# Splitting the probabilities and values of one attention branch into high and low parts

## The chip, the cores and the metric

The kernel runs on one core of one Trainium2 chip, in float32. The metric is the device time of one execution in microseconds (us); lower is better. The engines are TensorE (PE; PEld is its weight load), VectorE (DVE), ScalarE (ACT), GpSimd (POOL) and SyncE (SP), which here only issues DMAs. In the profile a matmul on float32r operands shows one weight load and one matmul, a matmul on float32 operands shows two of each, which are called two passes here.

## The reference

One layer of a streaming encoder on 1024 prompt tokens and 64 sample tokens, model width 1024. Two attention branches read one input projection; branch A is what is changed:

```python
_, idx = lax.top_k(score, topk)
k_sel = jax.vmap(lambda kb, ib: kb[ib])(k_all, idx)
v_sel = jax.vmap(lambda vb, ib: vb[ib])(v_all, idx)
...
logits = (jnp.einsum('bthd,btkd->bthk', qa, k_sel).astype(jnp.float32) * (HEAD_DIM ** -0.5)
          + jnp.moveaxis(bias, -1, 2))
logits = jnp.where(valid[:, :, None, :], logits, NEG_INF)
probs = jax.nn.softmax(logits, axis=-1).astype(v_sel.dtype)
return jnp.einsum('bthk,btkd->bthd', probs, v_sel)
```

Branch A has 8 query heads of width 64 that share one K and one V; each query keeps its 256 best keys. Branch B is a sliding-window attention with 8 heads. After them come the gates, the output projection, and a feed-forward block of width 4096.

## The kernel before

The kernel works in stages: input normalisation, indexer and top-k, input projection, branch A, branch B, output projection, feed-forward, final norm. Each engine has one instruction stream in program order, with semaphores between them.

Branch A is a list of units (`attention_units`). For each pair of heads there are 13: units 0 to 3 are head 0 with query blocks 4 to 7 (5 to 8 key tiles of 128), units 4 to 7 are both heads with blocks 0 to 3 (2, 4, 6, 8 tiles), units 8 to 11 are head 1 with blocks 4 to 7, and unit 12 is the sample block of both heads (17 tiles: 16 of the cache and one of its own). A pair so has 89 tiles, branch A has 4 pairs, 52 units and 356 tiles. Units are counted from 0 within a pair below.

For a unit, TensorE makes the logits (`logits`), VectorE adds the bias and finds the row maximum in one instruction (L1807), negates the maximum (L1820), ScalarE takes the exponential with that maximum as bias (`probs`, L1423), TensorE turns the probabilities with the identity in groups of up to four tiles (`turn_probs`, L1082) into PSUM bank 4 or 5, the turned group is copied to SBUF (`copy_turned`: even groups VectorE L1835, odd groups ScalarE L1439), TensorE multiplies it with the values (`weigh`, L1091; the turned probabilities are the stationary operand, the 64 value columns the moving one, both float32), and VectorE divides by the row sum into `y_tok` (`normalised`, L1868 to L1876).

In the loop iteration of unit n, TensorE turns unit n, makes the logits of unit n + 3, and weighs unit n - 1 (in the iteration of a sample unit, also that unit). A turn needs its PSUM bank free (`turn_read`), and a group is weighed when it has been copied. VectorE copies unit n, adds the bias for unit n + 3, takes the reciprocal of unit n, and normalises unit n - 1. ScalarE copies unit n and takes the exponential of unit n + 2.

The queries come through one buffer, `q_raw`, one head at a time. SyncE loads head hh (`load_q`, L500) when GpSimd has finished with the head before; ScalarE rounds it (`q_hi`, L1415) in its iterations of units 3 and 6 of a pair, at their end; GpSimd subtracts that from `q_raw` (L785) and so frees the buffer. GpSimd's loop over the 16 heads waits for nothing else within the first half of a pair.

At the end of the input projection VectorE copies the turned K and V rows out of PSUM into `kv_tok` (L1758), which TensorE waits for one group of products later (`beside_last`).

Of the kernel before, what the change touches and what calls it, by code (L numbers as in the profile page):

```python
# [5 lines left out]
F32 = mybir.dt.float32  # L6
# [7 lines left out]
P = 128  # L14
# [129 lines left out]
def hybrid_step(nc, x_prompt, x_sample, cache_k_a, cache_v_a, cache_kidx, cache_k_win, cache_v_win,  # L144
# [4 lines left out]
    with ExitStack() as ctx:  # L149
# [128 lines left out]
        probT = [at(f"probT{s}", [P, 4 * P], F32, B + (15168, 15680, 14016, 14528)[s]) for s in range(4)]  # L278
# [214 lines left out]
        def _(sp):  # L493
# [107 lines left out]
            def load_bias_a(pair):  # L601

                for half in range(2):
                    hh = 2 * pair + half
                    if pair:

                        sp.wait_ge(sem("biased"), starts[pair - 1] + (8, 12)[half])
# [3 lines left out]
            def load_bias_s(pair):  # L611

                if pair:
                    sp.wait_ge(sem("biased"), starts[pair])
# [28 lines left out]
            for dst_p, dst_s, tok, c0 in ((k_a_p, k_a_s, kv_tok, 0), (v_a_p, v_a_s, kv_tok, HD)):  # L643
                sp.dma_start(rows(dst_p), tok[:, 0:NBLK, c0:c0 + HD]).then_inc(stored, 16)
                sp.dma_start(dst_s[0, 0], tok[0:DEC, NBLK, c0:c0 + HD]).then_inc(stored, 16)
# [95 lines left out]
            sp.wait_ge(sem("out_stored"), 16 * 12)  # L741
# [3 lines left out]
        def _(pl):  # L745
# [36 lines left out]
            for hh in range(16):  # L782
# [5 lines left out]
                if hh % 2 == 1:  # L788
# [6 lines left out]
                    pl.wait_ge(sem("q_pair_done"), hh + 1)  # L795
            splits(4, 2, dmas=2)
# [5 lines left out]
        def _(pe):  # L802
# [211 lines left out]
            for name, v in (("tok_done", 4), ("kA_lo_done", 1), ("mask_ready", 1), ("cacheV_in", 16), ("cacheA_in", 32)):  # L1014
                pe.wait_ge(sem(name), v)
# [48 lines left out]
            def values(u, kb):  # L1064

                own = u["w"] - P * kb < P
                if u["br"] == "a":
                    tok = kv_tok[:, kb if u["blk"] is not None else NBLK, HD:P]
                    return tok[0:DEC] if own else (tok if u["blk"] is not None else cacheV[:, kb, :])
# [25 lines left out]
            def turn_outputs(pair, part):  # L1095
                pe.wait_ge(sem("y_done"), starts[pair + 1])
                for g, tl in units[starts[pair + 1] - 1]["turn"][part:part + 1]:
# [7 lines left out]
            def turn_outputs_a(n, pair, part):  # L1105

                pe.wait_ge(sem("y_done"), n - 1)
                for m, t in enumerate(units[starts[pair + 1] - 1]["turn"][part][1]):
# [13 lines left out]
            def weigh_all(u):  # L1122
# [7 lines left out]
                if u["n"] < 4:  # L1130
                    pe.wait_ge(sem("kAS_lo_done"), u["n"] + 1)
                for k, (g, before, tiles) in enumerate(groups):
# [127 lines left out]
        def _(ac):  # L1260
# [156 lines left out]
            def probs(u):  # L1417

                s = ring(u)
                ac.wait_ge(sem("biased"), u["n"] + 1)  # L1420
# [10 lines left out]
            def copy_turned(g, before, n):  # L1431

                if g % 2 == 0:
                    return
                ac.wait_ge(sem("turned1"), g // 2 + 1)
                free = before - 1 if g < a_groups else before
                if free > 0:
                    ac.wait_ge(sem("probT_used1"), free)
                ac.activation(probT[slot_of(g, before)][:, 0:n], bank(5, n), ACT.Copy).then_inc(sem("turn_read1"), 1)  # L1439

            def turn_hi_a(n, pair, part):

                if pair == 0 and part == 0:
                    ac.wait_ge(sem("out_stored"), 16 * 12)
# [106 lines left out]
        def _(dv):  # L1551
# [204 lines left out]
            for m, tok in ((0, kv_tok), (2, vb_tok)):  # L1756
                dv.wait_ge(sem("tok_turned"), m + 1)
                dv.tensor_copy(tok[:, 0:NBLK, :].rearrange("p t c -> p (t c)"), bank(6, 1024)).then_inc(sem("tok_done"), 1)  # L1758
                dv.wait_ge(sem("tok_turned"), m + 2)
                if m == 0:  # L1760
                    dv.tensor_copy(kb_tok[:, 0, :], bank(6)[:, P:2 * P])
# [10 lines left out]
            def inverse(u):  # L1772
# [3 lines left out]
                total = den if u["br"] == "b" else rsum  # L1776
# [287 lines left out]
```

## Time and profile before

| | us |
|---|---|
| median of 3 runs | 1857.34 (1856.16 to 1857.66) |
| the profiled execution | 1856.75 |
| its span, first to last instruction | 1854.8 |
| PE busy in the span | 1791.3 |
| DVE busy | 940.5 |
| ACT busy | 644.9 |
| POOL busy | 470.3 |

The span is what the profile covers; the rest of the profiled execution's time lies around it. Branch A takes the stretch from about 520 to 710 us. An engine's busy time says how long it had an instruction in work; whether it set the end is read from the stretch at issue.

### The profile page before, as it was taken

How to read it: one execution, taken by the hardware profiler on the slowest of the kernel's cores; microseconds unless marked ns; L12 is line 12 of the kernel's file. 1: busy time of each engine (PE TensorE's matmuls, PEld its weight loads, DVE VectorE, ACT ScalarE, POOL GpSimd, SP SyncE). 2: the span in 40 equal slices, each digit the busy share in tenths (PEclk: the TensorE clock that was granted, in tenths of full speed). 3: DMA queues.
4: the chain of work that ended last, by engine and by line, in shares of the span. 5: the costliest groups of instructions: out<-in, count | busy, mean ns of one | idle time of the engine just before them, and what ended most of it. 6: DMA issues, size and time to landing. Idle time of an engine off the chain costs nothing.

```text
span 1854.8 us, 30253 instructions
## 1 busy us (share of the span) xinstructions
PE 1791.3 (97%) x11176; PEld 1706.9 (92%) x11176; DVE 940.5 (51%) x2291; ACT 644.9 (35%) x1254; POOL 470.3 (25%) x269
## 2 busy tenths in 40 slices
PE   7799999999999998999999999999999999999996
PEld 2698999999989997779999999999999999999995
DVE  1657888899166665555645542333323232323234
ACT  3445666641255555453322240304030303121212
POOL 0521222224211110111223222323223333223330
PEclk9899999999999998999999999999999999999998
DMA  8510224342442234653441111111111111111112
GB/s 275 165 45 24 70 92 106 94 131 82 129 123 71 72 77 125 174 151 114 141 166 57 34 46 46 46 36 44 45 45 45 45 35 44 45 45 45 45 34 97
DMA packets 179321, 153.47 MB, mean 83 GB/s; under 512 B 20240, under 2 KB 162016, under 8 KB 178688
## 3 DMA queue, kind: packets, MB, share of 16 engines
q1 hardware_dynamic: 175328, 137.31, 25.9%
q10 hardware_dynamic: 3920, 15.19, 2.0%
q8 instruction: 47, 0.77, 0.2%
q14 instruction: 26, 0.21, 0.0%
HBM read 127.34 MB, written 25.19 MB: 82 GB/s over the span
## 4 chain that ended last, share of the span: by engine, by line
PE 89%; DVE 5%; ACT 3%; DMA 2%; issue 1%; POOL 0%; SPq 0%; ACTq 0%; DVEq 0%
PE psum L816 68%; PE psum L1091 5%; PE psum L1082 3%; PE psum L1118 3%; PE psum L940 2%; PE psum L973 2%; PE psum L1054 1%; PE psum L1055 1%; PE psum L854 1%; DVE h_f L1611 1%; PE psum L1058 1%; DVE u_lo L1996 1%; DMA out<-y_out 1%; DVE score L1668 1%; DMA ada_w<-in_w_ada 1%
## 5 line engine op out<-in xcount | busy, mean ns | idle before, releaser
L816 PE MATMUL psum<-h_hi,w_hi 128*128 128x362 f32 (+2 forms) x1440 | 475.1, 330 | 2.5 <-DVE h_lo L1974 1.6
L816 PE MATMUL psum<-h_lo,w_hi 128*128 128x362 f32 (+2 forms) x1440 | 474.5, 330 | 0.0
L816 PE MATMUL psum<-h_hi,w_lo 128*128 128x362 f32 (+2 forms) x1440 | 474.0, 329 | 0.0
L757 POOL CAST w_hi<-w_raw 128x1024 fp32r<-128x1024 f32 x112 | 124.9, 1115 | 1034.2 <-PEq L820 880.5
L759 POOL TENSOR_TENSOR w_lo<-w_raw,w_hi 128x1024 fp32r<-128x1024 f32 x112 | 281.7, 2515 | 9.0
L816 PEld LDWEIGHTS psum<-h_hi,w_hi 128*128 128x128 f32 x1440 | 271.6, 189 | 3.3 <-DVE h_lo L1974 1.9
L816 PEld LDWEIGHTS psum<-h_lo,w_hi 128*128 128x128 f32 x1440 | 271.9, 189 | 0.0
L816 PEld LDWEIGHTS psum<-h_hi,w_lo 128*128 128x128 f32 x1440 | 271.7, 189 | 0.0
L1958 DVE SCALAR_TENSOR_TENSOR xT<-psum,modT,xT 128x364 f32<-128x364 f32 (+3 forms) x288 | 136.0, 496 | 265.4 <-PE psum L816 265.4
L816 PE MATMUL psum<-u_hi,w_hi 128*128 128x362 f32 (+1 forms) x768 | 253.4, 330 | 3.2 <-DVE u_lo L1996 3.2
L1528 ACT ACTIVATE u_relu<-u_relu,b_up 128x364 f32<-128x364 f32 (+3 forms) x128 | 63.4, 519 | 553.5 <-DVE u_relu L2008 553.5
L816 PE MATMUL psum<-u_lo,w_hi 128*128 128x362 f32 (+1 forms) x768 | 252.0, 328 | 0.0
L816 PE MATMUL psum<-u_hi,w_lo 128*128 128x362 f32 (+1 forms) x768 | 251.7, 328 | 0.0
L816 PEld LDWEIGHTS psum<-u_hi,w_hi 128*128 128x128 f32 x768 | 144.4, 188 | 6.4 <-issue 4.9
L816 PEld LDWEIGHTS psum<-u_hi,w_lo 128*128 128x128 f32 x768 | 144.3, 188 | 0.0
L816 PEld LDWEIGHTS psum<-u_lo,w_hi 128*128 128x128 f32 x768 | 144.2, 188 | 0.0
L2008 DVE TENSOR_TENSOR u_relu<-psum,rstd_b 128x362 f32<-128x362 f32 (+1 forms) x96 | 51.1, 532 | 171.1 <-PE psum L816 171.1
L1689 DVE TENSOR_SCALAR_CACHE_REDUCE count_dump<-score,thresh 128x384 f32<-128x384 f32 (+4 forms) x160 | 130.6, 877 | 1.1
L785 POOL TENSOR_TENSOR q_hl<-q_raw,q_hl 64x1088 fp32r<-64x1088 f32 x16 | 40.1, 2503 | 276.7 <-ACT q_hl L1415 276.7
L1335 ACT ACTIVATE sign_dump<-score,thresh 128x1024 f32<-128x1024 f32 x64 | 102.2, 1600 | 19.3 <-DVE thresh L1685 19.3
L1317 ACT ACTIVATE z_out<-psum 128x362 f32<-128x362 f32 (+1 forms) x78 | 36.6, 469 | 152.0 <-PE psum L816 152.0
L1996 DVE TENSOR_TENSOR u_lo<-u_sq,u_hi 128x362 fp32r<-128x362 f32 (+1 forms) x96 | 75.4, 785 | 21.7 <-ACT u_hi L1533 9.4
(288 smaller groups left out, 2863.9 us busy)
## 6 DMA issues: line engine op xcount, KB each, us to landing
w_raw<-in_w_in SPq DMA_DIRECT2D x32, 512.0 KB, 4.1
ada_c<-in_w_ada SPq DMA_DIRECT2D x32, 512.0 KB, 4.0
w_raw<-in_w_up SPq DMA_DIRECT2D x32, 512.0 KB, 4.1
w_raw<-in_w_down SPq DMA_DIRECT2D x32, 512.0 KB, 3.5
zT_scratch<-z_out ACTq DMA_DIRECT2D x27, 544.0 KB, 2.7
q_raw<-zT_scratch SPq DMA_DIRECT2D x32, 272.0 KB, 5.1
gate<-zT_scratch SPq DMA_DIRECT2D x16, 544.0 KB, 4.6
ada_w<-in_w_ada SPq DMA_DIRECT2D x4, 2048.0 KB, 9.4
```

The costliest lines, as they stand in the source:

```text
L757: pl.tensor_copy(w_hi[slot][:, :], w_raw[slot][:, :]).then_inc(sem("w_hi_made"), 1)
L759: pl.tensor_tensor(w_lo[slot][:, :], w_raw[slot][:, :], w_hi[slot][:, :].bitcast(F32), ALU.subtract).then_inc(sem("w_split"), 1)
L816: ins = pe.matmul(bank(b, n), w[:, k, wc], x[:, a, c0:c0 + n], start=(m == 0 and p == 0), stop=(m == len(wk) - 1 and p == 2))
L1082: ins = pe.transpose(bank(4 + s, 512, slice(0, n))[:, m * P:m * P + P], buffer(u)[:, c:c + n], ident[:, :])
L1091: ins = pe.matmul(bank(6 + u["n"] % 2)[:, HD * lane:HD * lane + HD], probT[slot_of(g, before)][0:n, m * P:m * P + P], values(u, kb), start ...
L1118: ins = pe.matmul(ada_out_at(j), siluT[:, k::KT], ada_c[j % 2][:, k, :], start=(k == 0), stop=(k == KT - 1))
L1335: ins = ac.activation(sign_dump[g % 2][r, 0:c.stop - c.start], score[r, c], ACT.Sign, scale=-1.0, bias=thresh[r, g:g + 1].bitcast(F32), ac ...
L1528: ins = ac.activation(x, x, ACT.Relu, bias=b_up[:, d % 2, smp:smp + 1])
L1689: return dv.tensor_scalar(count_dump[r, c], score[r, c], th[r, g:g + 1].bitcast(F32), None, op, ALU.add, accum_out=count[r, g:g + 1])
L1958: ins = dv.scalar_tensor_tensor(x, ps if isinstance(m, int) else ps.unsqueeze(1), gt, x, ALU.mult, ALU.add)
L1996: dv.tensor_tensor(u_lo[:, d, c0:c0 + n], u_sq[:, k % 2, 0:n], u_hi[:, d, c0:c0 + n].bitcast(F32), ALU.subtract).then_inc(sem("u_done"), 1)
L2008: dv.tensor_tensor(u_relu[:, k % 2, 0:n], ps, rstd_b[:, c0:c0 + n], ALU.mult).then_inc(sem("u_scaled"), 1)
```

## The change

In branch A the turned probabilities are kept as two float32r tiles, `p_hi` (ScalarE rounds the turned group) and `p_lo` (VectorE subtracts `p_hi` from the turned group in PSUM), for every group. The values are kept as a pair of 64 columns, high and low, side by side: `vA` for the own tokens, made by VectorE beside the copy into `kv_tok`, and `vC` for the cache, made by GpSimd. `weigh` multiplies `p_hi` with all 128 columns and `p_lo` with the high 64. `normalised` divides the 128 columns into `y_raw` (two buffers), and GpSimd adds the halves into `y_tok` (`sum_parts`). The bias instruction gives the negative of the logits and their minimum, so that the separate negation goes, and the exponential has a scale of -1. On GpSimd the subtraction for the queries becomes `split_q`, and is put into a loop over the units: after the sum of unit 3 of a pair, and after that of unit 6. The stores of K and V are issued earlier on SyncE, and have their own semaphore.

```diff
-        kv_tok = at("kv_tok", [P, NT, P], F32, B + 2176)
+        kv_tok = at("kv_tok", [P, NT, P], F32, B + 16192)
+        vA = at("vA", [P, NT, 2, HD], F32R, B + 2176)
+        vC = at("vC", [P, 16, 2, HD], F32R, z_out_at)
...
+            sp.wait_ge(sem("tok_done"), 2)
+            for dst_p, dst_s, c0 in ((k_a_p, k_a_s, 0), (v_a_p, v_a_s, HD)):
+                sp.dma_start(rows(dst_p), kv_tok[:, 0:NBLK, c0:c0 + HD]).then_inc(sem("kv_stored"), 16)
+                sp.dma_start(dst_s[0, 0], kv_tok[0:DEC, NBLK, c0:c0 + HD]).then_inc(sem("kv_stored"), 16)
...
-            for hh in range(16):
+            def sum_parts(n):
+
+                u = units[n]
+                L = slice(0, u["lanes"])
+                y, raw = y_tok[pair_slot(u["pair"])], y_raw[n % 2]
+                pl.wait_ge(sem("y_done"), n + 1)
...
+                    ins = pl.tensor_tensor(y[:, u["blk"], c:c + HD * u["lanes"]].rearrange("p (l d) -> p l d", d=HD),
+                                           raw[:, L, 0, :], raw[:, L, 1, :], ALU.add)
+                ins.then_inc(sem("y_summed"), 1)
+                pl.wait_ge(sem("y_summed"), n + 1)
+
+            def split_q(hh):
+
                 q = q_hl[q_slot(hh)]
                 pl.wait_ge(sem("q_hi"), hh + 1)
                 pl.tensor_tensor(q[64:P, :], q_raw[64:P, ::-1], q[64:P, :].bitcast(F32), ALU.subtract)\
...
+            split_q(0)
+            split_q(1)
+            pl.wait_ge(sem("cacheV_in"), 16)
+            for slot in range(2):
+                pl.wait_ge(sem(f"z_stored{slot}"), 16 * 15)
+            pl.tensor_copy(vC[:, :, 0, :], cacheV[:, :, :]).then_inc(sem("vC_hi_done"), 1)
+            pl.wait_ge(sem("vC_hi_done"), 1)
+            pl.tensor_tensor(vC[:, :, 1, :], cacheV[:, :, :], vC[:, :, 0, :].bitcast(F32), ALU.subtract)\
+                .then_inc(sem("vC_done"), 1)
+            pl.wait_ge(sem("vC_done"), 1)
+            for u in units[0:NA]:
+                n = u["n"]
+                for past in weighed_at(n):
+                    sum_parts(past["n"])
+                for pair in range(4):
+                    for half in range(2):
+                        if n == min(starts[pair] + 4 + 3 * half, NA - 1):
+                            split_q(2 * pair + 2 + half)
+            for hh in range(10, 16):
+                split_q(hh)
...
+                if u["br"] == "a":
+                    for m, (lane, kb) in enumerate(tiles):
+                        n, v, out = min(P, u["w"] - P * kb), values(u, kb), bank(6 + u["n"] % 2)[:, P * lane:P * lane + P]
+                        pe.matmul(out, p_hi[slot_of(g, before)][0:n, m * P:m * P + P], v, start=(kb == 0), stop=False)
+                        ins = pe.matmul(out[:, 0:HD], p_lo[slot_of(g, before)][0:n, m * P:m * P + P], v[:, 0:HD],
+                                        start=False, stop=(kb == last))
+                    ins.then_inc(sem(f"probT_used{s}"), 1)
+                    return
...
+                if u["br"] == "a" and u["n"] >= 3:
+                    ac.wait_ge(sem("inverse_made"), u["n"] - 2)
                 for lane in range(u["lanes"]):
                     x = buffer(u)[:, lane_at(u, lane):lane_at(u, lane) + u["w"]]
-                    ins = ac.activation(x, x, ACT.Exp, bias=nmax[:, s, lane:lane + 1], accum_out=rsum[:, s, lane:lane + 1])
+                    ins = ac.activation(x, x, ACT.Exp, scale=-1.0, bias=nmax[:, s, lane:lane + 1], accum_out=rsum[:, s, lane:lane + 1])
...
+                if g < a_groups:
+                    ac.wait_ge(sem(f"turned{s}"), g // 2 + 1)
+                    if before > 1:
+                        ac.wait_ge(sem(f"probT_used{s}"), before - 1)
+                    ac.activation(p_hi[slot_of(g, before)][:, 0:n], bank(4 + s, n), ACT.Copy).then_inc(sem(f"p_hi_done{s}"), 1)
+                    return
...
+                    turned_v = bank(6, 1024).rearrange("p (t c) -> p t c", c=P)[:, :, HD:P]
+                    link(dv.tensor_copy(vA[:, 0:NBLK, 0, :], turned_v))
+                    dv.tensor_tensor(vA[:, 0:NBLK, 1, :], turned_v, vA[:, 0:NBLK, 0, :].bitcast(F32), ALU.subtract)
...
-                                                      in1=bias[:, c0:c0 + w], scale=1.0, scalar=-3e38, op0=ALU.add,
-                                                      op1=ALU.max, accum_out=mx[:, s, m + lane:m + lane + 1])
+                                                      in1=bias[:, c0:c0 + w], scale=-1.0, scalar=3e38, op0=ALU.add,
+                                                      op1=ALU.min, accum_out=low[:, m + lane:m + lane + 1])
...
+                if g < a_groups:
+                    dv.wait_ge(sem(f"p_hi_done{s}"), g // 2 + 1)
+                    x = slot_of(g, before)
+                    dv.tensor_tensor(p_lo[x][:, 0:n], bank(4 + s, n), p_hi[x][:, 0:n].bitcast(F32), ALU.subtract)\
+                        .then_inc(sem(f"turn_read{s}"), 1)
+                    return
...
+                    if n >= 2:
+                        dv.wait_ge(sem("y_summed"), n - 1)
```

## Rows read from the trace of the kernel before

**Rows 1.** The page: busy time by engine; the chain that ended last, by engine.
```profile
PE 1791.3 (97%) x11176; PEld 1706.9 (92%) x11176; DVE 940.5 (51%) x2291; ACT 644.9 (35%) x1254; POOL 470.3 (25%) x269
PE 89%; DVE 5%; ACT 3%; DMA 2%; issue 1%; POOL 0%; SPq 0%; ACTq 0%; DVEq 0%
```

**Rows 2.** Windows, 615 to 662; then VectorE's line L1807 alone there.
```profile
core 0: us, PE busy (x) PEld busy (x) DVE busy (x) ACT busy (x) POOL busy (x), PEclk, DMA share, GB/s
615.00:662.00 47.00, 46.92 (x363) 43.89 (x362) 30.32 (x96) 23.83 (x54) 5.43 (x4) 1.00 0.27 70
...
615.00:662.00 47.00, 14.48 (x38) 1.00 0.27 70
```

**Rows 3.** Timeline, last sample unit: start, length (us), engine, line, operands; [idle before].
```profile
705.39 0.61 PE L1082 MATMUL psum<-ident,logit_s 128*128 128x128 f32 x4
705.83 1.00 PE L1091 MATMUL psum<-cacheV,probT 128*128 128x64 f32 x8
706.03 0.60 ACT L1439 ACTIVATE probT<-psum 128x512 f32<-128x512 f32 x1 [2.91 <-PE psum L1082]
706.67 0.61 PE L1082 MATMUL psum<-ident,logit_s 128*128 128x128 f32 x4
707.11 1.00 PE L1091 MATMUL psum<-cacheV,probT 128*128 128x64 f32 x8
707.31 0.69 DVE L1835 COPY probT<-psum 128x512 f32<-128x512 f32 x1 [3.59 <-PE psum L1082]
```

**Rows 4.** Timeline of PE, two places with float32r matmuls.
```profile
621.36 0.27 PE L1055 MATMUL psum<-kA_lo,q_hl 128*128 128x128 f32 x1
621.47 0.28 PE L1060 MATMUL psum<-diag_r,swap_r 128*128 128x128 f32 x1
...
648.89 0.28 PE L1055 MATMUL psum<-kA_lo,q_pair 128*128 128x64 f32 x1
649.00 0.28 PE L1058 MATMUL psum<-selmask,swap_r 128*128 128x64 f32 x1
```

**Rows 5.** Lines by form, 615 to 662: count, busy us, mean ns, idle before.
```profile
L1835 DVE COPY probT<-psum 128x512 f32<-128x512 f32 x12 | 8.3, 688 | 3.5 <-PE psum L1082 2.9
L1876 DVE TENSOR_SCALAR y_tok<-psum,rden 128x64 f32<-128x64 f32 x8 | 2.2, 280 | 0.8 <-PE psum L1091 0.7
L1820 DVE TENSOR_SCALAR nmax<-mx 128x1 f32<-128x1 f32 x9 | 1.4, 153 | 0.0
L1841 DVE TENSOR_TENSOR yA_lo<-psum,yA_hi 128x384 fp32r<-128x384 f32 x2 | 1.1, 554 | 0.5 <-ACT yA_hi L1447 0.5
L793 POOL CAST q_pair<-q_hl 128x64 fp32r<-128x64 f32 x2 | 0.4, 238 | 0.1
```

**Rows 6.** Chain of waits in order of time: start, us, what.
```profile
500.04 3.95 PE psum L816 x24
```

**Rows 7.** Timeline, before the last sample unit: ScalarE and PE.
```profile
698.57 2.05 ACT L1423 ACTIVATE logit_s<-logit_s,nmax 128x2112 f32<-128x2112 f32 x1
...
701.88 1.04 PE L1082 MATMUL psum<-ident,logit_s 128*128 128x128 f32 x8
```

**Rows 8.** Timeline, third pair: the path of the queries, all engines.
```profile
630.02 2.50 POOL L785 TENSOR_TENSOR q_hl<-q_raw,q_hl 64x1088 fp32r<-64x1088 f32 x1 [35.65 <-ACT q_hl L1415]
...
632.55 1.10 SPq L500 DMA_DIRECT2D q_raw<-zT_scratch  x2
...
633.90 0.28 DVE L1876 TENSOR_SCALAR y_tok<-psum,rden 128x64 f32<-128x64 f32 x1 [0.16 <-PE psum L1091]
...
637.44 1.10 ACT L1415 ACTIVATE q_hl<-q_raw 128x1088 fp32r<-128x1088 f32 x1
639.11 0.60 ACT L1439 ACTIVATE probT<-psum 128x512 f32<-128x512 f32 x1 [0.57 <-PE psum L1082]
...
641.31 0.59 PEld L1082 LDWEIGHTS psum<-ident,logit 128*128 128x128 f32 x5
```

**Rows 9.** Tile q_raw, the two loads at 632.55 alone: time to landing.
```profile
DMA to landing us min/median/max: 3.5/3.8/4.1
```

More of the change, by code:

```diff
@@ L605, in load_bias_a @@
                     if pair:
-                        sp.wait_ge(sem("biased"), starts[pair - 1] + (8, 12)[half])
+                        sp.wait_ge(sem("piece_biased"), through(starts[pair - 1] + (8, 12)[half]))
                     sp.dma_start(biasA[half][:, :], bass.AP(relF, hh * RELS + REL0 - (SEQ - P) - (P - 1), [[1, P], [1, SEQ]]))\
@@ L613, in load_bias_s @@
                 if pair:
-                    sp.wait_ge(sem("biased"), starts[pair])
+                    sp.wait_ge(sem("piece_biased"), through(starts[pair]))
                 twice(lambda r: biasS[r, :],
@@ L1013, in _ @@
                 project_tile(q, between=lambda g, q=q: beside_last(q, g))
-            for name, v in (("tok_done", 4), ("kA_lo_done", 1), ("mask_ready", 1), ("cacheV_in", 16), ("cacheA_in", 32)):
+            for name, v in (("tok_done", 4), ("kA_lo_done", 1), ("mask_ready", 1), ("cacheA_in", 32)):
                 pe.wait_ge(sem(name), v)
@@ L1107, in turn_outputs_a @@
                 pe.wait_ge(sem("y_done"), n - 1)
+                pe.wait_ge(sem("y_summed"), starts[pair + 1])
                 for m, t in enumerate(units[starts[pair + 1] - 1]["turn"][part][1]):
@@ L1776, in inverse @@
                 total = den if u["br"] == "b" else rsum
+                if u["br"] == "a" and u["n"] >= 3:
+                    dv.wait_ge(sem("y_done"), u["n"] - 2)
                 dv.reciprocal(rden[:, s, L], total[:, s, L]).then_inc(sem("inverse_made"), 1)
@@ L1802, in biased @@
                     biases = [biasBS[:, u["pair"], :]]
+                low = nmax[:, s, :] if u["br"] == "a" and u["blk"] is not None else mx[:, s, :]
                 for m, (piece, c0, w) in enumerate(u["pieces"]):
@@ L1861, in normalised @@
                 dv.wait_ge(sem(f"probT_used{g % 2}"), before + 1)
+                if u["br"] == "a":
+                    if n == 0:
+                        dv.wait_ge(sem("kv_stored"), 16 * 4)
+                    if n >= 2:
+                        dv.wait_ge(sem("y_summed"), n - 1)
+                    raw = y_raw[n % 2]
+                    if u["blk"] is None:
+                        for half in range(2):
+                            r = slice(64 * half, 64 * half + 64)
+                            ins = dv.tensor_scalar(raw[0:DEC, half, :, :].rearrange("p h d -> p (h d)"), bank(6 + n % 2, P, r),
+                                                   rden[r, s, 0:1], None, ALU.mult)
+                    elif u["lanes"] == 2:
+                        ins = dv.tensor_tensor(raw[:, :, :, :].rearrange("p l h d -> p l (h d)"),
+                                               bank(6 + n % 2, 2 * P).rearrange("p (l d) -> p l d", l=2),
+                                               rden[:, s, :].unsqueeze(2).broadcast_to([P, 2, P]), ALU.mult)
+                    else:
+                        ins = dv.tensor_scalar(raw[:, 0, :, :].rearrange("p h d -> p (h d)"), bank(6 + n % 2, P),
+                                               rden[:, s, 0:1], None, ALU.mult)
+                    ins.then_inc(sem("y_done"), 1)
+                    return
                 j = n - NA
```

62 lines of the change are left out of this document (39 added, 23 removed).

## The prediction

> **What bounds the kernel now.** I read the page first, then the windows, then the chain, the lines by form and the timeline of one pair. On the page TensorE is busy for 97% of the span and holds 89% of the chain that ended last, VectorE for 51% [rows 1]. That is a mean over stages, so the stretch of branch A matters: in 615 to 662, one pair's worth of time, TensorE is busy 46.92 of 47.00 us, VectorE 30.32, ScalarE 23.83, GpSimd 5.43 [rows 2]. The granted clock is 1.00 there, so nothing is to be had from it. Each of the four pairs repeats this pattern. The reader is to see two things: a saving on VectorE or ScalarE is worth nothing here while TensorE stays full, and any new wait of TensorE is paid in full, because there is no idle time into which it could fall.
>
> **TensorE's own work.** Before, a tile of `weigh` is one float32 matmul of 64 columns, two passes. In the last sample unit eight passes go from 705.83 to 706.67, 0.105 us each [rows 3]. After, a tile is two float32r matmuls, one of 128 columns and one of 64. The trace has both with a new stationary operand each time: starts at 621.36 and 621.47 for 128 columns, at 648.89 and 649.00 for 64 [rows 4]. That is 0.11 us in both cases, whatever the columns: the time is set by loading the 128 by 128 weights, not by streaming. So a tile costs 2 x 0.105 = 0.21 us before and 2 x 0.11 = 0.22 after. Over 356 tiles that bounds the loss by 3.6 us; on the other side the two columns of starts are rounded to 0.01, so the same difference the other way, -3.6, is the bound for a gain. I take 0: the kinds of matmul repeat at the same step.
>
> The Trainium skill, FP8 and Floating Point Precision (section TensorE Precision Notes), states that true float32 takes four passes through the array. By it the change would take a tile from four passes to two, halve this work, and bring the sum to the third rival's time below. The trace disagrees: it shows two weight loads and two matmuls for a float32 tile, and the measurement decides.
>
> **VectorE and ScalarE.** In a pair there are 27 turned groups; VectorE copied 13 and ScalarE 14. Now ScalarE rounds all 27 and VectorE subtracts in all 27. ScalarE gains 13 at no more than 0.60 [rows 3], 7.8 us: at most 31.6 of 47. VectorE gains 14 at no more than 0.69; its subtraction from PSUM costs the same as a copy (384 columns 0.554, and 512 copied 0.688, a line through 0.13 for each 128) [rows 5]. That is 9.6 us. The normalisation is twice as wide: between 0 and its doubling, 13 x 0.28 = 3.6 [rows 5]. The negation goes, 9 x 0.153 = 1.4 [rows 5]. VectorE comes to at most 30.3 + 9.6 + 3.6 - 1.4 = 42.1 of 47. Both stay below TensorE, so in sum they cost nothing; the cover is TensorE's 46.9. The bias instruction with another scale and a minimum isn't in the trace; from below it costs what it does now, 14.48 us a pair [rows 2], from above twice that. I take the former, since its operands and width stay. The rounding of V at the end of the projection adds two passes of 512 columns from PSUM, 1.4 us, before `tok_done`; TensorE asks for that only after a further group of products, 3.95 us [rows 6]. The moved stores of K and V stand ahead of a wait for the last gate store on SyncE and cost nothing; the later DMAs of SyncE come earlier by them.
>
> **The longer chain of a group.** Turn, ScalarE, VectorE, TensorE now follow each other. For most units a whole iteration lies between turning and weighing. Only a sample unit has more than two groups, turned two groups ahead. There the turn that starts at 705.39 is copied by ScalarE from 706.03 to 706.63; a subtraction of 0.69 ends it at 707.35, and TensorE wants it at 707.11 [rows 3]: about 0.3 us late. The next one is copied from 707.31, so is ready at 708.6, where TensorE would be at 708.3: another 0.3. That is 0.6 for each sample unit, 1.8 for three pairs. In the last pair no logits lie between: ScalarE's long exponential ends at 700.62 [rows 7], now 0.5 later behind one more copy, then come two copies and two subtractions of unit 11. The turn of the sample unit, at 701.88 [rows 7], finds its banks free at about 702.45 and 703.05: 0.7 us, and of the unit's own 0.6 the first half is handed on to branch B, 1.0 together. Sum 2.8; bounds 0 (if TensorE's last group is late for other reasons anyway) and 5 (double).
>
> **The step that is moved.** GpSimd's subtraction for the queries stood in a loop of its own. Now it stands behind `sum_parts` of unit 3, which waits for `y_done` of that unit. What hangs on it: GpSimd frees `q_raw`, SyncE loads the next head, ScalarE rounds it at the end of its iteration of unit 6, and everything of ScalarE queues behind that, first the turned groups of unit 7. Before, in the third pair: GpSimd 630.02 to 632.52, SyncE's two loads from 632.55 [rows 8], the second about 0.5 later and landed 3.8 after its issue [rows 9], so at 636.9; ScalarE takes it at 637.44 without a wait [rows 8]. The margin is 0.5 us.
>
> After: unit 3 is normalised from 633.90 to 634.18 [rows 8]. Then the sum on GpSimd, which the trace doesn't have: from below the cast of 128x64, 0.24 [rows 5], from above the 2.50 of a subtraction with 17 times the columns [rows 8]; I take 0.35, near the former, as it has its size. The subtraction of 2.50 then ends at 637.1, not 632.5. The loads land 4.4 later, at 641.4. ScalarE rounds (1.10) until 642.5, copies the first group of unit 7 (0.60) until 643.15, VectorE subtracts (0.69) until 643.85. TensorE needs that bank to turn unit 8, for which it loads weights at 641.31 [rows 8]: 2.6 us late, and the second group some 0.2 more. I take 2.7. It comes once in each pair (heads 3, 5, 7 and 9), so 4 x 2.7 = 10.8. Bounds: with GpSimd's sum at 0.24 and no second wait 2.4 x 4 = 9.6; with a sum of 2.50 4.8 x 4 = 19. In the first pair the loads share the queue with others and ScalarE already waits, so its share is the least sure.
>
> What is late next: VectorE, in order, waits with ScalarE for the groups of unit 7, so the bias of unit 10 comes 3 us later; its exponential is two iterations ahead of its turn and takes that up. GpSimd's second subtraction of the pair moves as well, but its head is wanted only in the next pair.
>
> **Sum.** 10.8 + 2.8 + 0 = 13.6 on the profiled execution's 1856.75 (span 1854.8 and 1.95 around it): 1870.3, so 1870. That execution lies 0.6 below the median 1857.34, and within the runs.
>
> **Rivals.**
> First, the reload is hidden after all: if the loads land some 3 us earlier than I work out, or TensorE's order leaves it something to do. For it: ScalarE has idle time before its copies; against it: ScalarE's stream is in order and the bank is named in the wait. Then only 2.8 stays: 1859.6, with bounds 1856 to 1861.
> Second, VectorE becomes the bound. With the bias instruction at twice its price VectorE has 42.1 + 14.48 = 56.6 us a pair at the upper bounds, and 51 where the additions are at their middle (36.5); between them, at 53, a pair takes 53 in place of 47 + 2.7, and the time is 1870.3 + 4 x 3.3 = 1883. It decides from a bias instruction 1.5 times as long as now (42.1 + 7.6 = 49.7). Against it: the plain sum of 42.1 stays below 47.
> Third, faster: the short float32r passes cost less than the two places in [rows 4] tell, where each stands in a short run. If a tile fell to half, 0.105, TensorE would give back 356 x 0.105 = 37 us: 1833. The price at which it cancels the new waits is 0.17 a tile. For it: the streaming itself is short; against it: both widths repeat at 0.11 in the trace. The Trainium skill's four passes, cited above, would end here.
>
> **How the numbers follow.** Reload 0.62 (its own range 1865 to 1877), hidden 0.16, VectorE 0.15, faster 0.07. The range 1858 to 1880 holds the first, most of the hidden case and part of VectorE's. What a measurement of this kernel can tell from no change is about 0.2%, 3.7 us of 1857.34: 1853.6 to 1861.1. The third rival gives faster 0.07, the hidden case same 0.15, the rest is slower 0.78.
>
> **What would show it.** In the profile after: ScalarE's `q_hi` in iteration 6 of each pair waits about 4 us for the DMA of `q_raw`, and TensorE has one gap of 2 to 3 us before it turns unit 8; GpSimd's subtraction starts behind a sum, not behind `q_hi`; a short gap in each sample unit before its third and fourth group; the matmuls of `weigh` 0.11 apart; VectorE at 36 to 42 us of a pair. If branch A's pairs keep their 47 us, or `weigh` repeats at well under 0.1, I am wrong.

## The result, and the profile after

The changed kernel takes 1889.66 us (median of 4 runs, 1881.70 to 1898.52) against 1857.5 of the kernel before on the same chip: a ratio of 1.0174, 95% interval 1.0122 to 1.0227. It is slower, as forecast, but by 32 us and not by 13, and outside the range of 1858 to 1880. The profiled execution took 1881.70, with a span of 1879.9; it is the shortest of the four, so the trace shows 25 us of the loss.

The page, busy time and chain, beside [rows 1]:

```profile
PE 1801.5 (96%) x11176; PEld 1713.5 (91%) x11176; DVE 965.1 (51%) x2297; ACT 667.5 (36%) x1308; POOL 495.0 (26%) x323
PE 85%; DVE 5%; DMA 3%; ACT 3%; issue 2%; POOL 1%; SPq 0%; ACTq 0%; DVEq 0%; POOLq 0%
```

The busy shares hardly move. The chain says more: TensorE fell from 89 to 85%, and DMA, ScalarE, GpSimd and "issue" have come in, so that something now stops TensorE. Windows of the changed kernel: the stretch of [rows 2], and then one whole pair by its own length.

```profile
core 0: us, PE busy (x) PEld busy (x) DVE busy (x) ACT busy (x) POOL busy (x), PEclk, DMA share, GB/s
615.00:662.00 47.00, 42.32 (x319) 39.50 (x319) 30.56 (x89) 28.02 (x63) 7.15 (x14) 0.94 0.24 59
...
631.40:686.20 54.80, 50.02 (x365) 46.14 (x365) 35.75 (x97) 30.16 (x67) 10.28 (x17) 0.94 0.24 60
```

Two things changed against [rows 2]. TensorE is idle 4.7 us in 47, where it was idle 0.08. And the mean granted clock is 0.94, where it was 1.00: a part of the busy time is work at the lower of the two levels. A pair takes 54.8 us, where it took 47.3 (from the turn of the sample unit's last group in the second pair to that in the third: 616.82 to 664.09 before, 629.63 to 684.40 after).

The path of the queries in the third pair, from the chain of waits of the changed kernel in order of time (start, us, what); it answers to [rows 8]:

```profile
646.99 0.36 DVE y_raw L1962
...
647.49 0.33 POOL y_tok L800
...
647.89 2.52 POOL q_hl L809
...
650.42 0.47 SPq L505
...
650.93 5.81 DMA q_raw<-zT_scratch
...
656.76 0.02 ACT q_hl L1474
...
657.78 0.59 ACT p_hi L1502
...
658.39 0.70 DVE p_lo L1911
...
659.23 1.30 PE psum L1128 x5
```

This is the predicted path, step for step: the norm of unit 3, GpSimd's sum, its subtraction, SyncE's reload, ScalarE's rounding, then the turned group of unit 7, rounded and subtracted, and last TensorE's turn of unit 8. TensorE's gap stands before that turn, once in each pair (timeline of PE, the idle time in brackets):

```profile
549.92 0.84 PE L1128 MATMUL psum<-ident,logit 128*128 128x128 f32 x5 [3.06 <-DVE p_lo L1911]
604.29 1.30 PE L1128 MATMUL psum<-ident,logit 128*128 128x128 f32 x5 [4.37 <-DVE p_lo L1911]
659.23 1.30 PE L1128 MATMUL psum<-ident,logit 128*128 128x128 f32 x5 [4.46 <-DVE p_lo L1911]
713.27 1.30 PE L1128 MATMUL psum<-ident,logit 128*128 128x128 f32 x5 [3.73 <-DVE p_lo L1911]
```

15.6 us in sum. The turn behind the gap is the second thing to see: the same five matmuls take 0.84 behind the first gap and 1.30 behind the others. Windows around the third gap say why:

```profile
650.00:655.00 5.00, 4.76 (x38) 4.50 (x36) 2.24 (x6) 0.99 (x3) 1.32 (x3) 1.00 0.67 151
655.00:660.00 5.00, 0.77 (x4) 0.80 (x5) 1.61 (x3) 3.00 (x5) 0.00 (x0) 0.67 0.21 71
660.00:665.00 5.00, 5.00 (x26) 4.42 (x25) 3.19 (x9) 1.79 (x4) 3.37 (x4) 0.65 0.00 0
665.00:670.00 5.00, 4.90 (x31) 4.06 (x31) 4.11 (x11) 2.00 (x4) 0.46 (x1) 1.00 0.31 105
```

TensorE stands idle from 654.8, the granted clock falls from 1.00 to a mean of 0.67 in these five microseconds, and in the next five TensorE is busy throughout, but at 0.65: most of it at 1.2 GHz, not 2.4. In the kernel before there was no such spell inside branch A.

### The profile page after: what moved, and what is told of

It reads as the page before. It is cut to its first block, busy times and chain, and to the rows that moved or that the text cites. A ratio compares the mean times of both kernels' runs of the same rounds, so it can differ in the third digit from the quotient of the medians.

```text
span 1879.9 us, 30483 instructions
## 1 busy us (share of the span) xinstructions
PE 1801.5 (96%) x11176; PEld 1713.5 (91%) x11176; DVE 965.1 (51%) x2297; ACT 667.5 (36%) x1308; POOL 495.0 (26%) x323
## 4 chain that ended last, share of the span: by engine, by line
PE 85%; DVE 5%; DMA 3%; ACT 3%; issue 2%; POOL 1%; SPq 0%; ACTq 0%; DVEq 0%; POOLq 0%
PE psum L861 67%; PE psum L1128 3%; PE psum L1175 2%; PE psum L1138 2%; PE psum L985 2%; PE psum L1018 2%; PE psum L1139 1%; PE psum L899 1%; DMA q_raw<-zT_scratch 1%; PE psum L1099 1%; PE psum L1100 1%; DMA ada_c<-in_w_ada 1%; PE psum L1145 1%; DVE h_f L1681 1%; DVE u_lo L2100 1%
## 5 line engine op out<-in xcount | busy, mean ns | idle before, releaser
L1911 DVE TENSOR_TENSOR p_lo<-psum,p_hi 128x512 fp32r<-128x512 f32 (+3 forms) x108 | 60.3, 593 | 54.7 <-ACT p_hi L1502 54.3
```

Of the source, the lines that this page charges most:

```text
L1911: dv.tensor_tensor(p_lo[x][:, 0:n], bank(4 + s, n), p_hi[x][:, 0:n].bitcast(F32), ALU.subtract)\
```

## The experiments

The theory after the trace: the moved step of GpSimd costs nearly everything, once as the gap and once more as work at the lower clock behind it. The rival: the new work itself (two products a tile, a subtraction for every group, wider norms, sums) costs the rest. Periods below are those of the third pair, measured as above. Each ratio is to runs of the kernel before that were taken beside that experiment, and times of different experiments compare to within some 3 us; against the changed kernel itself, whose four runs are spread, to within some 10.

| kernel | time | ratio to before (95%) | period |
|---|---|---|---|
| before | 1857.1 to 1858.4 | 1 | 47.3 |
| changed | 1889.7 | 1.0174 (1.0122 to 1.0227) | 54.8 |
| split one unit earlier | 1861.8 | 1.0018 (1.0009 to 1.0027) | 48.5 |
| move alone, in the kernel before | 1875.7 | 1.0093 (1.0076 to 1.0109) | 51.3 |
| changed, gap filled | 1876.6 | 1.0090 (1.0075 to 1.0104) | 52.5 |
| earlier stores, in the kernel before | 1856.3 | 0.9982 (0.9973 to 0.9992) | 47.3 |
| changed, bias held | 1886.2 | 1.0141 (1.0120 to 1.0162) | 57.1 |
| split earlier, turn first | 1858.3 | 1.0000 (0.9991 to 1.0009) | 47.7 |
| the same, bias held | 1856.4 | 0.9989 (0.9977 to 1.0001) | 47.6 |
| split before the sum, turn first | 1856.4 | 0.9996 (0.9986 to 1.0005) | 47.4 |
| split earlier, no low product | 1845.4 | 0.9927 (0.9912 to 0.9941) | 42.5 |

### The split one unit earlier

```diff
-                        if n == min(starts[pair] + 4 + 3 * half, NA - 1):
+                        if n == starts[pair] + 3 + 3 * half:
```

> The changed kernel with GpSimd's split of the queries one unit earlier in its loop: after the sums of units 2 and 5 of a pair, not of units 3 and 6. Nothing else is changed. Theory (the reload): the one gap per pair came from the wait of GpSimd for the sum of unit 3, and the half clock from the gap. Then ScalarE finds q_raw loaded in the iteration of unit 6, TensorE has no gap of 4.5 us before the turn of unit 8, no stretch of branch A falls to the half clock, a pair takes 47 to 48.5 us where it took 54.8, and the time is 1857 to 1862. Rival (the new work itself: two products a tile, a subtraction for every group, wider norms, GpSimd's sums): the gap goes, but the groups stay late; a pair stays above 51 us and the time above 1873.

Measured: 1861.78, period 48.5. One line of the change gives back 27.9 of the 32 us (22.2 between the two profiled executions, 1881.70 and 1859.46). The windows of this kernel over one pair, and ScalarE's waits for `q_raw` in all of branch A (us, times, longest):

```profile
619.63:668.10 48.47, 48.09 (x364) 44.40 (x365) 35.66 (x97) 30.31 (x67) 10.28 (x17) 1.00 0.27 68
```

```profile
ACT q_hl L1474 <- DMA q_raw<-zT_scratch: 4.4, 4, 1.4
```

The clock is 1.00, TensorE is busy 48.09 of 48.47, and VectorE and ScalarE have the same work as in the changed kernel (35.66 and 30.31 against 35.75 and 30.16). So that work is not what sets the pace. The theory holds; ScalarE's wait shrinks from 5.8 to 1.4 but does not go, which was not expected.

### The move alone, in the kernel before

```diff
                 pl.wait_ge(sem("q_hi"), hh + 1)
+                if 2 <= hh < 10:
+                    pl.wait_ge(sem("y_done"), starts[hh // 2 - 1] + 4 + 3 * (hh % 2))
```

> The kernel before with the move alone: GpSimd's subtraction for heads 2 to 9 waits also until unit 3 (second head of the pair: unit 6) is normalised; no split of probabilities or values, no sums. Theory (the reload): the gap comes back without any of the rest, shorter by what the chain of a group lacks here (no sum of 0.33, one copy of 0.6 in place of a rounding and a subtraction): some 3 us a pair, with the half clock after it 5 to 6 in all, so 1872 to 1882. Rival (the move hurts only together with the longer chain of a group): under 1 us a pair, 1857 to 1861.

Measured: 1875.72, 17 us slower. The move alone brings the gap back, shorter than in the changed kernel, as expected: 9.7 us in sum over the four pairs. The clock falls behind three of the four gaps, those of 2.56 to 2.96, and not behind the first, of 1.41. The timeline of this kernel in the second pair: GpSimd begins when unit 3 is normalised, and TensorE waits for the turned group.

```profile
589.07 2.52 POOL L787 TENSOR_TENSOR q_hl<-q_raw,q_hl 64x1088 fp32r<-64x1088 f32 x1 [37.13 <-DVE y_tok L1878]
...
599.09 1.10 PE L1084 MATMUL psum<-ident,logit 128*128 128x128 f32 x5 [2.80 <-ACT probT L1441]
```

### The gap filled

```diff
+                if n < NA and n - starts[u["pair"]] == 8:
+                    pe.wait_ge(sem("y_done"), n - 2)
+                    for _ in range(19):
+                        pe.matmul(bank(6 + (n - 1) % 2, 512), kA_hi[:, 0:P], kA_hi[:, 0:512], start=True, stop=True)
```

> The changed kernel with 19 further products of 512 columns (some 0.23 each, 4.4 us) on TensorE in each pair, ahead of the turn of unit 8, where its gap is; they go to a bank that is free there and nothing reads them. The gap stays as long, but TensorE is busy in it. Theory (the gap costs twice, once itself and once in the half clock behind it): the granted clock stays at 1.00 through branch A, a pair goes from 54.8 to 51.5 to 52.5, the time to 1872 to 1878 and the runs lie within 3 us of each other. Rival (the half clock costs nothing because VectorE and ScalarE set the pace behind the gap): the pair stays within 0.5 us of 54.8 and the time at 1880 or more.

Measured: 1876.58, period 52.5, both as the theory has them. TensorE does useless work in the place of its gap, and the kernel gets 13.1 us faster by the medians. That is the price of the lower clock, 3.3 us a pair, apart from the gap: what is left above the first experiment is 14.8, 3.7 a pair. The size is rough. The third pair gets 2.3 us shorter (54.8 to 52.5), and of the 22.2 us between the profiled executions of the changed kernel and of the first experiment the gaps are 15.6, which leaves 6.6, or some 1.6 a pair. Windows of this kernel: the stretch of the third gap, then one behind the first sample unit.

```profile
650.00:655.00 5.00, 5.00 (x34) 4.55 (x32) 0.63 (x4) 1.15 (x2) 0.46 (x1) 1.00 0.82 216
655.00:660.00 5.00, 5.00 (x30) 4.25 (x28) 3.90 (x9) 3.64 (x8) 1.60 (x2) 1.00 0.00 0
...
570.00:575.00 5.00, 4.80 (x42) 4.38 (x41) 1.76 (x4) 1.47 (x3) 0.00 (x0) 1.00 0.00 0
575.00:580.00 5.00, 5.00 (x24) 4.23 (x24) 2.48 (x6) 1.86 (x5) 0.77 (x2) 0.66 0.02 5
```

Not all came as expected. The clock is 1.00 around the filled gap, but it fell at 575, behind short waits of the sample unit, and once more in the third sample unit (a mean of 0.71 in 680 to 685), so that the 13.1 still holds some work at the lower clock; and the runs lie 5.3 us apart, not 3.

### The earlier stores of K and V, in the kernel before

```diff
             load_q(1)
+            sp.wait_ge(sem("tok_done"), 2)
+            for dst_p, dst_s, c0 in ((k_a_p, k_a_s, 0), (v_a_p, v_a_s, HD)):
+                sp.dma_start(rows(dst_p), kv_tok[:, 0:NBLK, c0:c0 + HD]).then_inc(stored, 16)
+                sp.dma_start(dst_s[0, 0], kv_tok[0:DEC, NBLK, c0:c0 + HD]).then_inc(stored, 16)
...
-            for dst_p, dst_s, tok, c0 in ((k_a_p, k_a_s, kv_tok, 0), (v_a_p, v_a_s, kv_tok, HD)):
-                sp.dma_start(rows(dst_p), tok[:, 0:NBLK, c0:c0 + HD]).then_inc(stored, 16)
-                sp.dma_start(dst_s[0, 0], tok[0:DEC, NBLK, c0:c0 + HD]).then_inc(stored, 16)
```

> The kernel before with one other part of the change alone: the stores of K and V stand ahead of SyncE's wait for the last gate store. In the kernel before ScalarE waits 2.1 and 2.9 us for q_raw in the first pair and TensorE then 1.1 us. Theory: the later loads of SyncE's queue come earlier by the stores, the two waits shrink by some 2 us and the 1.1 us of TensorE goes: 1855.5 to 1857. Rival: the stores only move their traffic beside the loads of the first queries and the bias: no change, 1857 to 1859.

Measured: 1856.28, ratio 0.9982: 2 to 3 us faster, inside the range of the theory. ScalarE's waits for `q_raw` in the first pair fall from 2.1 and 2.9 us to 0 and 0.7. The prediction priced this part at nothing.

### The bias held until the reload has landed

```diff
                         sp.wait_ge(sem("piece_biased"), through(starts[pair - 1] + (8, 12)[half]))
+                        sp.wait_ge(sem("q_in"), 32 * (2 * pair + 2))
```

> The changed kernel with SyncE's load of the next pair's bias (512 KB, issued 1.1 us behind the reload of q_raw) held back until q_raw has landed. Theory (the reload landed 6.3 us after its issue, not 4.4, because it shares the DMA engines with that bias load): it lands 4 to 4.5 us after the issue, ScalarE's wait falls from 5.8 to some 4 us and TensorE's gap from 4.5 to 2.5 us; with the half clock behind it the time is 1876 to 1884, and under 1874 if so short a gap leaves the clock at 1.00. Rival (the landing is the two loads' own, 272 KB in rows of 4 KB): the gap stays at 4 us or more and the time at 1887 or more.

Measured: 1886.19, between the two expectations, and its interval overlaps that of the changed kernel. Tile `q_raw`, the two loads of the third pair, time to landing (min, median, max), first in the changed kernel and then in this one; [rows 9] had 3.5, 3.8, 4.1:

```profile
DMA to landing us min/median/max: 3.7/4.7/5.8
```

```profile
DMA to landing us min/median/max: 3.7/4.2/4.7
```

The second load is the one that decides. It takes 5.8 beside the bias load and 4.7 without it, and TensorE's gap in this pair is 3.40 instead of 4.46. But the bias load is not shown to be the cause. In the second pair, held as well, the load still takes 5.3 (5.7 in the changed kernel), and in the last, which has no bias load behind it, 5.3 against 5.1. And the kernel before and the first experiment have the same bias load 0.7 and 0.6 us behind the second load, which takes 4.1 there and 4.5. SyncE in these two kernels, and the landing of the first experiment's two loads:

```profile
633.77 11.70 SPq L608 DMA_DIRECT2D biasA<-rel_bias_scratch  x2
...
636.68 10.50 SPq L613 DMA_DIRECT2D biasA<-rel_bias_scratch  x2
...
DMA to landing us min/median/max: 3.6/4.1/4.5
```

What the slow landings have in common is something else. The second loads of the four pairs of branch A, in all thirteen traces, are 52. In eleven of them one packet of 16 KB, of the DMA queue that the profile lists as q8 instruction, begins within 2.5 us of the load's issue, and these take 4.7 to 5.8; the other 41 take 4.1 to 4.6, but for one of 5.0, whether a bias load follows or not. The packet in the changed kernel, in 650.93 to 653.43:

```profile
q8 instruction: 1, 0.02, 2.8%
```

No run moves this packet by itself, so it is a lead and not a shown cause. The hold brings little time back: TensorE's four gaps are still 14.4 us in sum, and the clock still falls. Here it stayed low longer (a mean of 0.53, 0.50 and 0.60 in 655 to 660, 660 to 665 and 665 to 670), which is how the period of this pair comes to be 57.1 with a shorter gap.

### The turn first in the sample units

On top of the earlier split:

```diff
-                    weigh(u, g, before, tiles)
                     if k + 2 < len(groups):
                         turn_probs(u, groups[k + 2][0], groups[k + 2][2])
+                    weigh(u, g, before, tiles)
```

> The kernel with the earlier split, and in a sample unit TensorE turns group k + 2 before it weighs group k (both wait for the same release of the bank), so that the chain of turn, ScalarE, VectorE has 0.85 us more. Theory (what is left of the loss is the longer chain of a group in the four sample units, some 0.3 us twice in each): TensorE's two waits in a sample unit go, 0.6 a unit, 4 x 0.6 = 2.4 us less than the kernel with the earlier split: 1858.5 to 1860. Rival (those waits are covered elsewhere, or the rest lies in the change from float32r products to float32 turns): within 0.7 us of it.

Measured: 1858.30, 3.5 below the first experiment (some 1 to 6 by the intervals), where 2.4 was expected. The waits that it removes, in the timeline of the first experiment's kernel, third sample unit; it answers to [rows 3]:

```profile
664.61 0.65 PE L1128 MATMUL psum<-ident,logit_s 128*128 128x128 f32 x4
664.63 0.69 DVE L1911 TENSOR_TENSOR p_lo<-psum,p_hi 128x512 fp32r<-128x512 f32 x1 [2.38 <-ACT p_hi L1502]
...
665.37 0.33 PE L1138 MATMUL psum<-vC,p_hi 128*128 128x128 f32 x1
...
666.29 0.30 PE L1128 MATMUL psum<-ident,logit_s 128*64 128x128 f32 x1
```

VectorE's subtraction ends at 665.32 and TensorE weighs at 665.37. From the turn at 664.61 to the next at 666.29 are 1.68 us, where [rows 3] has 1.28 (705.39 to 706.67). With the turn first the same two turns stand 1.30 apart (662.79 and 664.09).

### The bias held as well, and the split before the sum

Both on top of the turn first. The hold of the bias is that of the experiment above; the split before the sum:

```diff
+                for pair in range(4):
+                    for half in range(2):
+                        if n == starts[pair] + 3 + 3 * half:
+                            split_q(2 * pair + 2 + half)
                 for past in weighed_at(n):
                     sum_parts(past["n"])
-                for pair in range(4):
...
```

> The kernel before this one (earlier split, turn first in the sample units) with the next pair's bias also held back until q_raw has landed. With the earlier split ScalarE still waits about 1.1 us for q_raw in each pair and TensorE 0.2 to 0.3 after it. Theory: the wait of ScalarE goes, another 1 us in all, so 1857 to 1859, level with the kernel before; as far as the earlier stores of K and V give 2 us, this stays behind the kernel before with those stores alone (1856.3). Rival: the hold makes the bias late in the next pair and costs 2 us or more.

> The kernel with the earlier split and the turn first in the sample units, with GpSimd's split of the queries now also ahead of the sum of unit 2 (unit 5), so that it waits for ScalarE's rounding alone, as in the kernel before. With the earlier split GpSimd began 1.7 us after that rounding, ScalarE still waited 1.4 us for q_raw and TensorE 0.2 for the turned group. Theory: both waits go, 0.2 to 0.3 us a pair, 1857 to 1858. Then branch A of the changed kernel costs no more than that of the kernel before with the same stores (1856.3), within some 1.5 us. Rival: the sums of units 2 and 5 now come 2.5 us later, hold up a norm and with it TensorE: 1859 or more.

Measured: 1856.44 and 1856.39, periods 47.6 and 47.4. Neither is told apart from the other or from the kernel before, and neither beats the kernel before with the earlier stores alone. In the second, ScalarE's waits for `q_raw` over all of branch A are all but gone, which shows that GpSimd's wait for the sum of unit 2 was what the first experiment had left:

```profile
ACT q_hl L1474 <- DMA q_raw<-zT_scratch: 0.4, 1, 0.4
```

### No low product

On top of the earlier split, one product of 128 columns a tile:

```diff
-                        pe.matmul(out, p_hi[slot_of(g, before)][0:n, m * P:m * P + P], v, start=(kb == 0), stop=False)
-                        ins = pe.matmul(out[:, 0:HD], p_lo[slot_of(g, before)][0:n, m * P:m * P + P], v[:, 0:HD],
-                                        start=False, stop=(kb == last))
+                        ins = pe.matmul(out, p_hi[slot_of(g, before)][0:n, m * P:m * P + P], v, start=(kb == 0), stop=(kb == last))
```

> The kernel with the earlier split (first experiment), without the product of the low part of the probabilities with the high part of the values: one product of 128 columns a tile in place of two; the low parts are still made by VectorE, and nothing reads them. So the result lacks that term. Theory (TensorE's passes cost 0.107 us each by weight load and TensorE sets the pace): 89 passes fewer a pair are 9.5 us, less what VectorE (36 of 48 us busy) and the chain of a group then hold back: a pair takes 39 to 42 us, the time 1826 to 1838. Rival (the short float32r passes are cheaper than 0.107, or the products lie beside something else): a pair stays above 44 us, the time above 1845.

Measured: 1845.43, 16 us less than with both products, at the rival's edge, although the theory's price is right. Timeline of PE in this kernel, a unit of 8 tiles and what follows; then its waits of TensorE and ScalarE in branch A (us, times, longest):

```profile
607.30 1.00 PE L1138 MATMUL psum<-vA,p_hi 128*128 128x128 f32 x8
608.14 0.28 PE L1138 MATMUL psum<-vC,p_hi 128*128 128x128 f32 x1
```

```profile
PE psum L1128 <- DVE p_lo L1909: 12.4, 6, 2.7
...
ACT q_hl L1472 <- DMA q_raw<-zT_scratch: 11.6, 4, 3.0
```

Eight passes take 0.84, 0.105 each, with nothing else between them. What failed is the rest of the expectation: it counted on VectorE and the chain of a group, and forgot the reload. When TensorE does an iteration faster, the loads land late again, ScalarE waits up to 3.0 us, and TensorE's wait for the turned group is back. The granted clock falls with it: means of 0.81 in 545 to 550, 0.74 in 590 to 595 and 0.78 in 675 to 680, and 0.50 from 695 on, before branch B begins. That is read from this trace; no run takes these waits away.

### The passage to branch B filled

The kernel before with the earlier stores, and the changed kernel with turn first and bias held; `keep_busy` makes products of 128 columns into a free bank:

```diff
                     ins.then_inc(sem("kwin_turned"), 1)
+                    keep_busy(32)
                     pe.wait_ge(sem("kB_lo_done"), 2)
...
+                if n == NA:
+                    keep_busy(13)
                 pe.wait_ge(sem("probs_made"), n + 1)
```

> The kernel before with the earlier stores, and at the passage from branch A to branch B 32 products of 128 columns (0.107 each, 3.4 us) where TensorE waits 3.5 us for the low part of branch B's keys, and 13 (1.4 us) where it waits 1.5 us for the first exponential; they go to a bank that is free there and nothing reads them. In the kernel before the granted clock falls there to half of full speed and comes back after some 12 us. Theory (an idle TensorE costs a second time in the half clock behind it, here as in the gap of the changed kernel): the clock stays at 1.00 there, the some 7 us of work at the half clock take half, as far as TensorE sets the pace there: 2 to 4 us less than with the earlier stores alone, 1852 to 1854.5. Rival (VectorE, ScalarE and the loads set the pace at the passage): within 1 us of 1856.3.

> The same products at the passage in the changed kernel with the earlier split, the turn first in the sample units and the bias held. Theory: the same 2 to 4 us less as in the kernel before: 1852.5 to 1854.5, and so no further apart from the kernel before with the same products than 1856.4 is from 1856.3. Rival: within 1 us of 1856.4.

Measured: 1856.20 (ratio 0.9993, 0.9985 to 1.0002) and 1857.01 (0.9991, 0.9980 to 1.0001): the rival, twice. Windows of the passage, first with the earlier stores alone, then filled:

```profile
710.00:714.00 4.00, 1.26 (x6) 1.26 (x7) 3.64 (x4) 0.05 (x1) 0.00 (x0) 0.79 0.66 183
714.00:718.00 4.00, 2.53 (x12) 2.23 (x12) 3.48 (x18) 2.17 (x11) 0.00 (x0) 0.50 1.07 246
718.00:722.00 4.00, 4.00 (x20) 2.28 (x18) 1.40 (x9) 3.28 (x15) 0.00 (x0) 0.50 0.30 75
```

```profile
710.00:714.00 4.00, 4.00 (x36) 3.86 (x36) 3.55 (x4) 0.74 (x2) 0.00 (x0) 1.00 0.47 122
714.00:718.00 4.00, 2.68 (x24) 2.54 (x24) 3.57 (x16) 1.47 (x7) 0.00 (x0) 1.00 1.04 257
718.00:722.00 4.00, 3.86 (x34) 3.12 (x34) 1.81 (x13) 4.00 (x19) 0.00 (x0) 1.00 0.51 129
```

The clock did what was expected, 1.00 where it was 0.50, and the time did not follow: here VectorE (3.6 of 4), the loads (a share of 1.0) and then ScalarE (4.00 of 4) set the pace.

## Why the prediction was wrong

**TensorE's own work: right.** A tile was to cost the same before and after. In the first experiment's kernel the 16 passes of a unit with 8 tiles take 1.70 us (633.22 to 634.92), in the kernel before 1.73 (631.90 to 633.63). The rival "faster" is out: a pass takes 0.105 to 0.108 in the float32 form, at 128 columns (the run without the low product) and, over such a unit, in the mixture of 128 and 64. In the sample units the mixture takes a little more, 0.90 for four tiles (663.71 to 664.61, first experiment) where 0.84 stood, near the 0.22 a tile of the prediction's bound. The four passes that the prediction set against the trace are not refuted by it. At 512 columns the kernel before comes near them: a float32 matmul there has two records 0.43 apart, 0.86 in all, and a float32r one has 0.23 to the next start:

```profile
28.30 7.03 PE L854 MATMUL psum<-ada_w,siluT 128*2 128x512 f32 x16
...
666.33 0.40 PE L1055 MATMUL psum<-kA_lo,q_hl 128*128 128x512 f32 x1
666.56 0.39 PE L1058 MATMUL psum<-selmask,swap_r 128*128 128x512 f32 x1
```

At the 64 and 128 columns of `weigh` a record takes its 0.105 to 0.11 whatever its columns, so nothing was to be gained there.

**VectorE and ScalarE: right.** VectorE has 35.7 us a pair, just under the 36 to 42 foreseen, ScalarE 30.2 under its 31.6. The bias instruction costs 14.42 in a pair (L1887, first experiment) against 14.48 [rows 2], so the second rival is out. With the queries and the sample units put right the split values take 1856.4 (the split before the sum), and the earlier stores without them 1856.3; by the ratios, 0.9996 and 0.9982, they cost some 3 us, by the periods, 47.4 and 47.3, 0.1 or 0.2 a pair. No gain shows, and a small cost is not out.

**The longer chain of a group: right.** 2.8 us predicted. The third sample unit, from its first turn to the next unit's, takes 9.47 us in the first experiment (658.55 to 668.02), 8.71 in the kernel before and 8.75 with the turn first: 0.7 where 0.6 was predicted. The run with the turn first gives back 3.5 by the medians, and the wait in the last pair, which it leaves, is 0.4.

**The moved stores: a miss of the other sign.** Priced at nothing, they are worth 2 to 3 us by themselves.

**The step that is moved: the step that failed.** Place, cause, direction and the chain of events were right. Its size was 10.8 us and is 27.9, the difference between the changed kernel and the one with the split one unit earlier (22.2 in the profiled executions). One term was too small, and one was left out.

First, the gap itself: "I take 2.7" stands against 3.1 to 4.5, 15.6 us in the four pairs, inside the prediction's own bounds of 9.6 to 19 for this term. The chain from the end of the norm to the turn was worked out at 9.7 us and took 11.9 (647.35 to 659.23 in the third pair). Nearly all of that is the landing, 4.4 us behind SyncE's first issue by the prediction and 6.3 in the trace (650.42 to 656.74). Of these 1.9 us, 0.3 were misread in [rows 9]: the second load's time is the 4.1 and not the median 3.8. The rest stays open: holding the bias load took 1.1 off in this pair, but the kernel before has that load behind its own 4.1, and the packet named above is only a lead.

Second, the lower clock behind each gap, 6.6 us in the profiled executions and 13.1 by the medians, which the prediction put at nothing: "any new wait of TensorE is paid in full" priced a wait by its own length. This is the term that carries the time out of the range. With the gaps at their measured 15.6 and no price for the clock the sum is 15.6 + 2.8 + 1856.75 = 1875.2, inside it. Its sentence "nothing is to be had from it", of a granted clock of 1.00, saw a gain only and not what there was to lose. The trace of the kernel before showed the price at another place, the passage to branch B, in windows that the prediction did not use:

```profile
708.00:710.00 2.00, 1.89 (x15) 1.48 (x13) 0.55 (x4) 1.74 (x2) 0.00 (x0) 1.00 0.01 4
710.00:712.00 2.00, 0.00 (x0) 0.00 (x0) 1.74 (x2) 0.72 (x2) 0.00 (x0) 0.68 0.05 15
712.00:716.00 4.00, 2.59 (x12) 2.59 (x12) 3.44 (x8) 0.00 (x0) 0.00 (x0) 0.50 0.99 240
716.00:720.00 4.00, 2.53 (x12) 1.76 (x12) 3.22 (x20) 3.50 (x17) 0.00 (x0) 0.50 1.09 252
720.00:724.00 4.00, 4.00 (x32) 3.02 (x31) 1.33 (x10) 2.52 (x10) 0.00 (x0) 0.88 0.16 43
```

TensorE stops for some 3.5 us, the clock falls to 0.50 and comes back only some ten microseconds later. A new gap of 2.7 us in a stretch where TensorE sets the pace should have been priced with a tail of that kind: with the 3.3 us a pair that were then measured by the medians, 4 x (2.7 + 3.3) + 2.8 + 1856.75 is 1883.6, beside a median of 1889.66; the gap's own miss, 4.8 us, makes up most of what is left. The Trainium skill, TensorE: Matmul & The Clock Gate (section HAM oscillation — how this bites in real kernels), describes a kernel whose wait for a DMA returns with every tile, so that each tile begins at the lower clock and the loss is paid every time. The trace agrees, with 0.67 and 0.65 around the third gap; it was the rule to weigh, and it was not weighed.

The four runs spread over 17 us for the same reason, as far as their mean clocks tell: 1881.70 has 0.982, 1884.90 has 0.981, 1894.42 has 0.977 and 1898.52 has 0.975.

## What to carry to other kernels

A step that frees a buffer should wait for nothing but its own input: put behind another step in an in-order queue, it takes on that step's waits, and the buffer's next load and every engine behind that load inherit them. Where one engine is full, price a new gap twice, the idle time and the work at the lower clock that follows, and read the second price from any gap that the trace already has; at a place where other engines set the pace, as at the passage to branch B here, no second price could be measured.

## What the runs showed of the hardware that was not expected

- The lower clock also came where only short waits stood ahead of it. With the gap filled, TensorE was busy 4.80 of 5 us before 575, and the next 5 us ran at 0.66. In 625 to 630 of the same run, and in 665 to 670 of the first experiment's, it was busy the same 4.80 of 5, in the same place of a sample unit, and the clock stayed at 1.00. What made the difference is open.
- How long the lower clock lasted differs for one and the same gap. From the means of the windows (a mean of 0.67 over 5 us is 3.3 us at half) it was some 3.4 us behind the first gap of the changed kernel (0.66 in 550 to 555), some 7 around its third and nearly 14 with the bias held, although the gap was shorter there.
- One and the same load of 272 KB landed 4.1 to 5.8 us behind its issue in these traces. A load of 512 KB right behind it did not decide which (4.1 to 4.6 with and without one); the slow ones go with a packet of the instruction queue in their first 2.5 us.
